# Last expert's w_down by column halves with the next block's first projection among them, and k_dil moved between the turns and the first scores

## The reference

```python
def expert_choice_moe(h, w_router, b_router, w_gate_e, w_up_e, w_down_e):
    ...
    a = jnp.einsum('becd,edf->becf', xe, w_gate_e)
    u = jnp.einsum('becd,edf->becf', xe, w_up_e)
    y = jnp.einsum('becf,efd->becd', jax.nn.silu(a) * u, w_down_e)
    y = y * vals[..., None]
    return zeros((s, d)).at[idx].add(y)

# end of the first block
x = rms_norm(x + gate_f * moe_out, g_final)
# second block
h = rms_norm_2(x, mix_norm_g)
dq, dk, dv, bq, bk, bv, z = split(h @ w_in)          # q_diff k_diff v_diff q_dil k_dil v_dil z
a = diff_attention(rms(dq), rms(dk), dv)             # softmax(...) of two maps, w = a0 - lam * a1
b = dilated_attention(rms(bq), rms(bk), bv)
x = x + (concat(a, b) * silu(z)) @ w_out
x = x + sigmoid(rms_norm_2(x) @ w_ple_gate) * (p @ w_ple_proj)
```

## Time and profile before

| | us |
|---|---|
| median of three runs | 1310.07 |
| the profiled execution, its own time | 1309.2 |
| its span | 1307.4 |
| last slot of w_down reaches PE at | 1124.92 |
| PE busy / DVE busy / ACT busy | 978.1 / 385.5 / 247.1 |
| mean rate of the loads | 380 GB/s |

### The profile page before, as it was taken

How to read it: one execution, slowest core, us unless ns; L and a number is a source line. 1 busy time by engine, 2 the same in 40 slices (tenths; PEclk the granted TensorE clock), 3 DMA queues, 4 the chain that set the end, 5 groups by cost and what they waited for, 6 DMA issues and landing times.

```text
span 1307.4 us, 15592 instructions
## 1 busy us (share of the span) xinstructions
PE 978.1 (75%) x6744; PEld 559.2 (43%) x6744; DVE 385.5 (29%) x590; ACT 247.1 (19%) x376; POOL 21.3 (2%) x47
## 2 busy tenths in 40 slices
PE   9999999968565665646666656666665675899998
PEld 7899998323121221212122121212121221478988
DVE  5888866200010110000011000001010000488865
ACT  4454434000000000000000000000000000467744
POOL 2000200000000000000000000000000000000000
PEclk9999999999778878788778787879788878999999
DMA  9998999999999999999999999999999999965230
GB/s 337 389 386 326 314 384 420 401 429 431 426 430 433 432 431 432 425 432 437 428 430 431 429 430 438 431 428 430 431 430 435 431 433 418 397 226 164 95 129 33
DMA packets 70204, 496.43 MB, mean 380 GB/s; under 512 B 4842, under 2 KB 27002, under 8 KB 49680
## 3 DMA queue, kind: packets, MB, share of 16 engines
q1 hardware_dynamic: 67840, 489.11, 90.6%
q0 software_dynamic: 2080, 6.55, 1.6%
q10 hardware_dynamic: 240, 0.11, 0.0%
HBM read 494.71 MB, written 1.06 MB: 379 GB/s over the span
## 4 chain that ended last, share of the span: by engine, by line
DMA 56%; PE 39%; SPq 2%; DVE 1%; issue 1%; ACT 0%; DVEq 0%
DMA ring<-in_w_down_e 23%; DMA ring<-in_w_up_e 18%; DMA ring<-in_w_gate_e 15%; PE psum L748 8%; PE psum L750 8%; PE psum L749 8%; PE psum L1217 7%; PE psum L1247 4%; SPq L571 1%; PE psum L1258 1%; SPq L584 1%; DMA ring<-in_w_in 1%; PE psum L1300 1%; PE psum L1194 1%; PE psum L1335 0%
## 5 line engine op out<-in xcount | busy, mean ns | idle before, releaser
L1217 PE MATMUL psum<-ring,arena 128*32 128x512 f32 x2048 | 300.4, 734 | 186.1 <-DMA ring<-in_w_up_e 109.8
L1247 PE MATMUL psum<-ring,arena 128*32 128x512 f32 x976 | 158.8, 777 | 104.6 <-DMA ring<-in_w_down_e 103.9
L1217 PEld LDWEIGHTS psum<-ring,arena 128*32 128x32 f32 x2048 | 69.4, 129 | 377.5 <-issue 168.5
L1247 PEld LDWEIGHTS psum<-ring,arena 128*32 128x32 f32 x976 | 41.5, 132 | 205.2 <-issue 136.9
L1849 DVE TENSOR_TENSOR ring_r<-ring,ring_r 128x2048 fp32r<-128x2048 f32 x49 | 111.1, 2288 | 35.8 <-ACT ring_r L1458 35.6
L1626 ACT ACTIVATE arena<-psum 128x512 f32<-128x512 f32 x16 | 9.6, 598 | 532.1 <-PE psum L1217 532.1
L748 PE MATMUL psum<-ht_hi,ring_r 128*128 128x256 f32 x384 | 108.5, 283 | 0.0
L750 PE MATMUL psum<-ht_hi,ring_r 128*128 128x256 f32 x384 | 107.3, 279 | 0.0
L749 PE MATMUL psum<-ht_lo,ring_r 128*128 128x256 f32 x384 | 107.2, 279 | 0.0
L2211 DVE TENSOR_TENSOR arena<-psum,arena 128x512 f32<-128x512 f32 x32 | 20.6, 686 | 291.8 <-PE psum L1247 291.8
L1458 ACT ACTIVATE ring_r<-ring 128x2048 fp32r<-128x2048 f32 x49 | 92.5, 1910 | 29.7 <-PE psum L750 22.6
(11 more groups left out here) (307 smaller groups left out, 934.1 us busy)
## 6 DMA issues: line engine op xcount, KB each, us to landing
ring<-in_w_gate_e SPq DMA_DIRECT2D x23, 4096.0 KB, 33.3
ring<-in_w_up_e SPq DMA_DIRECT2D x22, 4096.0 KB, 33.3
ring<-in_w_down_e SPq DMA_DIRECT2D x21, 4096.0 KB, 33.9
ring<-in_w_up_e SPq DMA_DIRECT2D x16, 2048.0 KB, 36.3
ring<-in_w_in SPq DMA_DIRECT2D x31, 1024.0 KB, 9.9
ring<-in_w_gate_e SPq DMA_DIRECT2D x14, 2048.0 KB, 36.5
ring<-in_w_down_e SPq DMA_DIRECT2D x14, 2048.0 KB, 36.9
ring<-in_w_ada SPq DMA_DIRECT2D x16, 1024.0 KB, 9.8
```

The lines of the kernel that those rows point to most:

```text
L1217: last = mm(psum[32 * g:32 * g + 32, b, :].rearrange("s (q c) -> s q c", c=4), cur[h][:, k, :], w[:, g // 2, :, g % 2 * 4:g % 2 * 4 + 4], ...
L1247: last = mm(psum[32 * q:32 * q + 32, 2 + n, :], act_t[:, f % 4, (f // 4) * CAP:(f // 4 + 1) * CAP], w[:, kk, n * BANK:(n + 1) * BANK], sta ...
```

## The change

1. The last expert's w_down comes in eight slots by column halves: four slots hold the left 512 columns of all its rows, then four the right ones. A slot of 1 MB is now read in pieces of 512 float32 (2 KB); before it was 2048 in one piece (8 KB). Each of its four products goes to a strip of its own. Between the first three slots PE gets fillers (`keep_busy`, products of 128 columns whose result nobody reads), four each, and two behind the fourth.
2. Between the two halves SP loads q_diff's first weight slot, to a place of its own (`tail_room[0]`). PE does the scatter of the left half, then pair 0 of q_diff, two slots of w_down, pair 1, two slots, the scatter of the right half (y by quarters), then pair 2 (now column by column) and pair 3. q_diff's second slot is loaded and split in halves too.
3. The bias is loaded behind q_diff's second slot.
4. k_dil comes before scale_row and the first scores; the second scores come behind v_diff. ACT's and DVE's lists are put in another order around it.
5. w_out's first quarter comes before turn_cat1. Its last product goes row tile by row tile, so that `add_half` and the turning can begin with the first one. Units wait for one bank, then the other, not for both.

```diff
-TAIL_UNITS = [..., ("turn_k_diff", 0), ("turn_q_diff", 0), ("scale_row", 0), ("k_dil", 2),
+TAIL_UNITS = [..., ("turn_k_diff", 0), ("turn_q_diff", 0), ("k_dil", 2), ("scale_row", 0),
...
-SCORES_AFTER = {"scale_row": 0, "k_dil": 1, "turn_w1": 2, "turn_e0b": 3}
+SCORES_AFTER = {"scale_row": 0, "v_diff": 1, "turn_w1": 2, "turn_e0b": 3}
...
+            def load_last_down(j):
+                n, block, part = j // 4, j % 4 // 2, j % 2
+                rows = t["w_down_e"][0][NE - 1].rearrange("(b p k) n -> b p k n", b=2, k=KD)[block]
+                at = expert_place(last_down + j)
+                sp.wait_ge(slot_used, HEAD_SLOTS + released(last_down + j))
+                sp.dma_start(shaped(ring[:, at, :], k=4, n=BANK), rows[:, 4 * part:4 * part + 4, n * BANK:(n + 1) * BANK]).then_inc(loaded[at], 16)
...
+            for j in range(4):
+                load_last_down(j)
+            sp.wait_ge(slot_used, FIRST_TAIL - RING + 1)
+            load_entry(0)
+            for j in range(4, 8):
+                load_last_down(j)
...
-            pool.wait_ge(slot_used, first_slot["q_diff"] + 1)
+            pool.wait_ge(slot_used, first_slot["q_diff"] + 2)
...
+            def last_down(j):
+                n, at = j // 4, expert_place(NE * EXPERT_SLOTS - 8 + j)
+                arrived(pe, FIRST_TAIL - 8 + j)
+                w = shaped(ring[:, at, :], k=4, n=BANK)
+                for kk in range(4):
+                    f = 4 * (j % 4) + kk
+                    last = mm(psum[32 * kk:32 * kk + 32, 2 + n, :], act_t[:, kk, (f // 4) * CAP:(f // 4 + 1) * CAP], w[:, kk, :],
+                              start=(f < 4), stop=(f >= 12), tile_position=(0, 32 * kk))
+                return last
...
+            for j in range(4):
+                last_down(j).then_inc(slot_used, 1)
+                keep_busy(4 if j < 3 else 2, 3)
+            pe.wait_ge(y_ready, 2 * NE - 1)
+            scatter(0)
+            scatter(1)
+            entry_pair(0)
+            last_down(4).then_inc(slot_used, 1)
+            last_down(5).then_inc(slot_used, 1)
+            entry_pair(1)
+            last_down(6).then_inc(slot_used, 1)
+            last_down(7).then_inc(slot_used, 2)
+            for half in range(2):
+                pe.wait_ge(y_ready, 2 * NE + half)
+                scatter(2 + half)
...
+                if name == "pv_dil1":
+                    pe.wait_ge(scores_read, 16)
+                    out_product(0)
+            for i in range(1, 4):
                 out_product(i)
```

ACT's list:

```diff
             unit("turn_q_diff")
+            head_root(2)
             split("v_diff", 0)
+            split("v_diff", 1)
+            unit("k_dil")
             unit("scale_row")
-            head_root(2)
-            split("v_diff", 1)
+            split("v_dil", 0)
+            head_root(3)
             exponentials(0)
-            split("v_dil", 0)
-            unit("k_dil")
             split("v_dil", 1)
-            exponentials(1)
-            head_root(3)
             unit("v_diff")
             split("z0", 0)
+            exponentials(1)
             split("z0", 1)
             unit("v_dil")
```

DVE's list:

```diff
-            split("k_dil", 1)
             scale_x()
             unit("turn_k_diff")
+            split("k_dil", 1)
+            unit("turn_q_diff")
             qk_sums(2)
-            unit("turn_q_diff")
+            split("v_diff", 0)
+            qk_rows(2)
+            split("v_diff", 1)
+            unit("scale_row")
             score_rows(0)
-            split("v_diff", 0)
-            unit("scale_row")
             score_max(0)
-            split("v_diff", 1)
-            qk_rows(2)
+            qk_sums(3)
             split("v_dil", 0)
+            lambda_sums()
+            qk_rows(3)
+            split("v_dil", 1)
+            diff_weights(0)
+            unit("v_diff")
             score_rows(1)
             score_max(1)
-            split("v_dil", 1)
-            qk_sums(3)
-            lambda_sums()
-            diff_weights(0)
-            unit("v_diff")
-            qk_rows(3)
             diff_weights(1)
             unit("v_dil")
```

More of the change, by code:

```diff
@@ L92 @@
 STEPS, STEP_K = 4, 2
-TAIL_UNITS = [("q_diff", 2), ("k_diff", 2), ("q_dil", 2), ("turn_k_diff", 0), ("turn_q_diff", 0), ("scale_row", 0), ("k_dil", 2),
+TAIL_UNITS = [("q_diff", 2), ("k_diff", 2), ("q_dil", 2), ("turn_k_diff", 0), ("turn_q_diff", 0), ("k_dil", 2), ("scale_row", 0),
               ("v_diff", 2), ("v_dil", 2), ("turn_w0", 0), ("turn_k_dil", 0), ("turn_q_dil", 0), ("turn_w1", 0), ("pv_diff", 0),
@@ L851, in columns_rows, with rows_product @@
                 last.then_inc(slot_used, 1)
-            def rows_product(s, u, await_pair=None):
+            def rows_product(s, u, sems=None):
                 for i in range(2):
                     w = split_slot(s + i, k=FG, n=BANK)
[L857 to L866, removed]
-                        if await_pair and i and pair == 0:
-                            turn_stream_back()
-                    last.then_inc(slot_used, 1)
@@ L871, in begin @@
-            def begin(sems, u):
-                for j in range(2):
+                    for tt in range(TT):
+                        if i == 0 and tt and sems is not None:
+                            begin(sems, u, (1,))
+                        for kk in range(FG):
+                            k = FG * i + kk
+                            last = split_product(bank(2 * (u % 2) + tt), [a[:, k, tt * P:(tt + 1) * P] for a in (ht_hi, ht_lo)],
+                                                 [h[:, kk, :] for h in w], k == 0, k == KD - 1)
+                        if k == KD - 1 and tt == 0:
+                            end_first(last)
@@ L1195, in side_step, with scatter @@
                         last.then_inc(pp_done, 1)
+            def scatter(q):
+                for c in range(2):
+                    k = 2 * q + c
+                    last = mm(bank(4 + q, c=2, s=SEQ)[:, c, :], y[:, k // 4, k % 4 * P:(k % 4 + 1) * P], gwt.rearrange("p t m -> p (t m)"),
+                              start=False, stop=True, skip_group_check=True)
+                last.then_inc(scattered, 1)
+            def last_down(j):
[6 more added lines that the diff above has]
+                              start=(f < 4), stop=(f >= 12), tile_position=(0, 32 * kk))
+                return last
             def expert(i, h, looped=False, side=False):
@@ L1239, in expert @@
                 pe.wait_ge(cur_ready, 2 * i + (h + 2))
+                if not looped and i == NE // 2 - 1 and h == 1:
+                    return
                 for j in range(8):
@@ L1255, in expert @@
                     for q in (2 * n, 2 * n + 1):
-                        for c in range(2):
-                            at = (2 * q + c) * P - n * BANK
-                            last = mm(bank(4 + q, c=2, s=SEQ)[:, c, :], y[:, n, at:at + P], gwt.rearrange("p t m -> p (t m)"),
-                                      start=False, stop=True, skip_group_check=True)
-                        last.then_inc(scattered, 1)
+                        scatter(q)
                 if side:
```

156 lines of the change are left out of this document (100 added, 56 removed).

## The result

| | before | changed |
|---|---|---|
| median of 12 runs each, us | 1309.76 (1309.09 to 1311.43) | 1313.99 (1312.46 to 1318.64) |
| profiled execution, span, us | 1307.4 | 1311.1 |

What follows compares the result with a forecast made beforehand. It took weight transfers to bound the kernel until w_down's last slot, then PE's nearly unbroken tail. Order loss 2.1 plus clock 1.1 minus end 0.75 gave +2.4 on 1310.07: 1312.4 us, range 1305.0 to 1315.0.

Steps and rivals of the forecast that it cites:

- The chain: Small DVE and ACT work from first scores through second `diff_weights`: 33.4 us, then DVE's copy of v_dil to 34.2.
- S: Start of the first scores, forecast at 1177.3; later steps are counted from it, the third scores at +36.5.
- the stall stays away: Rival before turn_k_dil: the chain reaches DVE's copy before v_dil ends, all gains stand, 1305.3; chance 0.20.
- the clock holds: Rival behind the stall: PE stalls, but the burst in its middle keeps the clock up, 1311.4; chance 0.15.
- the short pieces starve PE: Rival at the entry: loads at 366 GB/s bring w_down's last slot 1.4 later, 1313.8; chance 0.20.
- The entry, 2.6: From w_down's slots to the turning after q_diff's pair 2: the turning starts 2.6 us earlier.
- The fillers fit into the gaps between arrivals, also nothing: At the entry: filler matmuls between w_down's slots run while PE waits for loads, costing nothing.
- PE is not late: At w_down's last slot: PE's earlier work is done at about 1128.7, before the slot arrives at 1129.3.
- the loads, is late: Rival at the entry: PE rather than loads is late; 1 us more work costs 0.4; no separate chance.
- Until the first scores, 4.0: Gain up to the first scores: 2.6 from the entry, 0.4 at the turns, 1.0 from an idle gone.
- The clock, 1.1: Behind the stall before turn_k_dil: turns at half speed cost 1.1 us, bounds nothing to 1.65.
- The end, 0.75: At turn_cat1: w_out's early quarter saves 0.65 and single banks about 0.1; row order nothing.

Runs made afterwards that it cites:

- e2: The kernel before with only the new order of k_dil and the scores; ratio 1.0058 against before.
- e4: The changed kernel with only DVE's list reordered, among others the copy of v_dil before the second diff_weights; ratio 0.9994 against the kernel before.
- e3: The changed kernel with ACT's copy of v_dil and DVE's copies of v_dil and turn_w0 moved earlier; ratio 1.0012 against the kernel before.
- f1: The changed kernel without the 14 filler matmuls between w_down's first four half slots; 1313.84 us, ratio 1.0034 against the kernel before.
- f3: The changed kernel with the old order of k_dil and the scores, and no fillers; 1309.46 us, ratio 0.9993 against the kernel before.
- f4: The changed kernel with 32 filler calls on PE in the stall before turn_k_dil; ratio 1.0026 against the kernel before.
- g4: The kernel before with DVE's copies of turn_k_diff and turn_q_diff moved earlier and w_out's first quarter before turn_cat1; ratio 0.9990 against before.
- g1: The changed kernel with old scores order, no fillers, and DVE's copies of turn_k_diff and turn_q_diff moved earlier; 1305.32 us, ratio 0.9959 against before.
- e1: The changed kernel with only the order of k_dil and the scores put back; 1311.31 us, ratio 0.9998 against the kernel before.
- f2: The changed kernel with DVE's list reordered as in e4 and no fillers; 1308.18 us, ratio 0.9987 against the kernel before.
- g2: The kernel before with only DVE's copies of turn_k_diff and turn_q_diff moved earlier; ratio 0.9994 against before.
- g3: f2 with DVE's copy of turn_w0 moved ahead of the second diff_weights; ratio 0.9990 against the kernel before.

## Why the prediction was right, and where it was off

**Right: the sign and the mechanism.** The chain was forecast to reach S + 33.4 and the copy of v_dil to end at S + 34.2; they came at 33.2 and 34.0 (1211.30 and 1212.05, with S = 1178.08). The stalls were forecast at 5.3 and 1.3 and came at 4.96 and 0.56, with the releasers that were named; the second is short because the first half, at half clock, took 1.12 instead of 0.45. e2 shows that the order alone makes this loss, and e4 that cutting the chain removes it. The rival "the stall stays away" is refuted by the changed kernel's own trace, "the clock holds" by its stretches. The rival "the short pieces starve PE" gave 1313.8, nearer to the measured median than the forecast's 1312.4, but by luck: it needed 366 GB/s, and the pieces came at 383 to 391.

**Off by size, term by term**, on the profiled execution (forecast +2.4, measured +3.7):

- *The entry, 2.6.* Measured 2.0, or 1.7 by the distance from w_up's last slot (34.5 to 32.9). The step that failed is "The fillers fit into the gaps between arrivals, also nothing", and with it "PE is not late" for the last slot. The rate of the pieces was near the forecast's 388 (383 to 391 GB/s), but PE was later than the loads. The step holds in e3, where PE kept full clock: 31.9, the 2.6 of the forecast. It fails when PE comes late to w_down, as in the profiled execution, whose last slot of w_up took 3.31 instead of 1.92: that costs 1.0 by the distance, and where w_down starts at half clock as well up to 2.5 more (35.4 against 32.9). The rival "PE, not the loads, is late" named this and priced it at 0.4. How many executions it hits was not measured, and f1, without fillers, was no faster.
- *Until the first scores, 4.0.* In the new order S was forecast at 1177.3 and came at 1178.08, 0.6 of it the entry's. But the sentence that with k_dil behind the scores the gain "is" also 4.0 was wrong: f3 gained 0.1 there. I read the idle of 0.97 as a wait for one copy and did not ask whether DVE could do that copy sooner. So the new order had a use that I had not priced, it hides DVE's queue, and then it loses more at the next place.
- *The clock, 1.1.* Measured 2.1 in this trace (by f4); 1.4 behind the same stall in f1. I took 3.3 us of low clock from the earlier trace rows; here it lasted 6.
- *The end, 0.75.* Measured 1.2 (the distance from the third scores to the last turning fell from 66.45 to 65.24): 0.8 from w_out, by g4. The other 0.4 is put down to the waits on single banks, which I had at 0.1; no run took them alone.

Together 2.4 + 0.8 + 0.9 - 0.45 = 3.65, where 0.8 is S, 0.9 the way from S to the third scores (forecast 36.5 + 1.1, measured 38.5) and 0.45 the end.

The Trainium skill, "DMA: Bandwidth & Descriptors", section Specifications, lets 2 KB pieces run at full rate; the changed kernel's stretch 1114 to 1118 shows 387 GB/s against 422, so the measurement stands against it again. In the changed kernel's trace that costs nothing, because PE was the later one. Where PE was on time (e3, f1, f3, g1), the fourth half slot waited 0.27 to 1.52 for its load, so there the rate counts: an estimate is 0.2 for each of four slots, from the 2.49 and 2.70 of the prediction. No run loaded the halves at the higher rate. The bias load's move showed nothing and was not tried alone.

## What to carry to other kernels

Before moving a block of matmul work, ask what small work on the other engines it covers, and add up that chain in the order of each engine's queue: cover taken from one place is missing at the next. An idle of a matmul engine "for a copy" may be a full queue on the copying engine; then an earlier start gains nothing until that queue is reordered, which costs no instruction (f3, then g1). And work put in to keep an engine busy is free only while that engine waits for something anyway; once it is the late one, the fillers lie on the path. The traces show this here; the times do not settle what it cost.

## What was not expected of the hardware

- After the stall of about 5 us the granted clock stood near 0.5 for about 6 us (1210.4 to 1216.5), through a burst of four transposes and the work behind it. In f1, behind the same stall, it was back sooner (0.96 from 1215 to 1217). After an idle of 3.49 it had been 3.31.
- At the same place of the program, w_down's first slot, the clock was 1.00 in seven traces (before, changed, e2, e3, f1, f4, g4) and 0.50 in seven (e1, e4, f2, f3, g1, g2, g3). What decides it was not found. With the fillers it was passed on (35.0 and 35.4 to the turn back in e1 and e4); where loads leave slack it hardly was (31.9 to 32.2 in f2, f3, g1 and g3, 34.8 in g2).
